# Softmax division folded into the transposition of the probabilities: a diagonal matrix as the moving operand of a matmul

## The reference, cut to what matters

```
def fox_mix(u, q_norm_g, k_norm_g, fgate_b):
...
    for blk in range(s // BLOCK_Q):
        s0, s1 = blk * BLOCK_Q, (blk + 1) * BLOCK_Q
        scores = jnp.einsum('bqhd,bkhd->bhqk', q[:, s0:s1], k[:, :s1]) * scale
        bias = c[:, :, s0:s1, None] - c[:, :, None, :s1]
        causal = jnp.arange(s1)[None, :] <= (s0 + jnp.arange(BLOCK_Q))[:, None]
        scores = jnp.where(causal, scores + bias, -jnp.inf)
        probs = jax.nn.softmax(scores, axis=-1)
        outs.append(jnp.einsum('bhqk,bkhd->bqhd', probs, v[:, :s1]))
```

## Time and profile before

| | |
|---|---|
| median of 3 runs | 2901.72 us (2898.87 to 2904.9) |
| the profiled execution's own time | 2899.26 us |
| its span | 2897.3 us |
| mean granted TensorE clock | 0.985 of 2.4 GHz |
| busy | PE 2782.7 us (96%), DVE 1161.8 (40%), ACT 1001.3 (35%), POOL 216.3 (7%) |

### The profile page before, as it was taken

The page is one execution under the profiler, slowest core; times in us unless marked ns, Lnnn a source line. Parts: engine busy times, 40 slices in busy tenths (PEclk is TensorE's granted clock), DMA queues, the critical chain, the costliest instruction groups (busy, mean ns, idle before and its releaser), DMA issues.

```text
span 2897.3 us, 41123 instructions
## 1 busy us (share of the span) xinstructions
PE 2782.7 (96%) x15562; PEld 2206.9 (76%) x15562; DVE 1161.8 (40%) x1677; ACT 1001.3 (35%) x1388; POOL 216.3 (7%) x343
## 2 busy tenths in 40 slices
PE   7989998998998979999999999999999999999998
PEld 5777676666666747888888888888888888888787
DVE  6643652553453343333333333333333333334544
ACT  5433533433442333343322333223332222233521
POOL 2100110120120011100000000000000000001300
PEclk9999999999999989999999999999999999999999
DMA  4221121112113104222223332233222322223332
GB/s 159 87 67 55 56 78 51 62 51 81 48 60 87 67 30 162 99 102 94 99 83 97 106 100 95 84 97 108 94 94 85 103 101 99 97 82 100 104 123 76
DMA packets 107733, 255.33 MB, mean 88 GB/s; under 512 B 35657, under 2 KB 37193, under 8 KB 107625
## 3 DMA queue, kind: packets, MB, share of 16 engines
q1 hardware_dynamic: 106352, 249.73, 26.9%
q0 software_dynamic: 1280, 4.20, 0.4%
HBM read 244.90 MB, written 8.98 MB: 88 GB/s over the span
## 4 chain that ended last, share of the span: by engine, by line
issue 75%; PE 14%; POOL 3%; DVE 2%; ACT 1%; SPq 0%; DMA 0%; POOLq 0%; DVEq 0%; ACTq 0%
PE bank L288 4%; PE bank L285 4%; PE bank L289 3%; PE bank L320 2%; POOL probs L971 1%; POOL scratch_pool L116 1%; SPq L1187 0%; DVE w_lo L280 0%; PE bank L470 0%; DMA solved_scratch<-solved 0%; POOL acc_e L1740 0%; POOL carried L994 0%; POOL sg_t L963 0%; POOL M_t L980 0%; PE bank L442 0%
## 5 line engine op out<-in xcount | busy, mean ns | idle before, releaser
L280 DVE TENSOR_TENSOR w_lo<-raw,w_hi 128x1024 fp32r<-128x1024 f32 (+1 forms) x476 | 541.8, 1140 | 963.5 <-ACT w_hi L273 953.5
L273 ACT ACTIVATE w_hi<-raw 128x1024 fp32r<-128x1024 f32 (+1 forms) x476 | 468.2, 987 | 1044.5 <-PE bank L289 999.2
L285 PE MATMUL bank<-hn_hi,w_hi 128*128 128x512 f32 x1664 | 648.1, 389 | 0.0
L289 PE MATMUL bank<-hn_hi,w_lo 128*128 128x512 f32 x1664 | 647.3, 389 | 0.0
L288 PE MATMUL bank<-hn_lo,w_hi 128*128 128x512 f32 x1664 | 647.3, 389 | 0.0
L285 PE MATMUL bank<-in_hi,w_hi 128*128 128x512 f32 x1086 | 467.3, 430 | 55.2 <-DMA T_t<-solved_scratch 31.2
L288 PE MATMUL bank<-in_lo,w_hi 128*128 128x512 f32 x1086 | 442.4, 407 | 0.0
L289 PE MATMUL bank<-in_hi,w_lo 128*128 128x512 f32 x1086 | 428.8, 395 | 0.0
L288 PEld LDWEIGHTS bank<-hn_lo,w_hi 128*128 128x128 f32 x1664 | 312.4, 188 | 65.3 <-issue 0.5
L285 PEld LDWEIGHTS bank<-hn_hi,w_hi 128*128 128x128 f32 x1664 | 312.4, 188 | 65.1 <-issue 0.5
L289 PEld LDWEIGHTS bank<-hn_hi,w_lo 128*128 128x128 f32 x1664 | 312.4, 188 | 64.9
(11 more groups left out here) (233 smaller groups left out, 2161.7 us busy)
## 6 DMA issues: line engine op xcount, KB each, us to landing
raw<-w_gu SPq DMA_DIRECT2D x176, 512.0 KB, 3.4
raw<-w_mix SPq DMA_DIRECT2D x136, 512.0 KB, 3.6
raw<-w_down SPq DMA_DIRECT2D x64, 384.0 KB, 3.1
raw<-w_down SPq DMA_DIRECT2D x64, 320.0 KB, 2.8
raw<-ple_gate SPq DMA_DIRECT2D x32, 512.0 KB, 3.5
x_raw<-xT SPq DMA_DIRECT2D x4, 1024.0 KB, 11.6
h_t<-xT SPq DMA_DIRECT2D x4, 1024.0 KB, 8.8
out<-h_t POOLq DMA_DIRECT2D x16, 256.0 KB, 2.3
```

What stands on the lines that cost most here:

```text
L273: nc.scalar.activation(w_hi[:, ring_slots(par2, half), 0:cols[half]], raw[:, half, 0:cols[half]], ACT.Copy).then_inc(hi_ready, 1)
L280: nc.vector.tensor_tensor(w_lo[:, s, 0:cols[half]], raw[:, half, 0:cols[half]], w_hi[:, s, 0:cols[half]].bitcast(F32), ALU.subtract).then_ ...
L285: nc.tensor.matmul(out, w_h, x_hi, start=start, stop=False, skip_group_check=True)
L289: return nc.tensor.matmul(out, w_l, x_hi, start=False, stop=stop, skip_group_check=True)
```

## The change

The DVE, right behind the reciprocal, writes `shares`: the identity times the reciprocals, one per row, so a 128x128 matrix with the reciprocal row sums on its diagonal (doubled, `q % 2`). The PE multiplies each block of unscaled probabilities by it in an ordinary float32 matmul where it transposed against the identity: the block is the stationary operand as before, and `shares` takes the identity's place as the moving one. The scaling on Pool is gone, in the groups and behind them. Nothing else is moved; line numbers from L204 on shift by one or more.

```
+    shares = sb("shares", [P, 2, P])
...
-            pe.wait_ge(S("probs_normed"), 16 * gp + q + 1)
+            pe.wait_ge(S("shares_ready"), 16 * gp + q + 1)
...
-                last = nc.tensor.transpose(pt_bank[q % 2][:, tok(kb)], probs[:, q % 2, tok(kb)], const(C_ID))
+                last = nc.tensor.matmul(pt_bank[q % 2][:, tok(kb)], probs[:, q % 2, tok(kb)], shares[:, q % 2, :],
+                                        start=True, stop=True)
...
             nc.vector.reciprocal(small[:, 12 + q % 2:13 + q % 2], small[:, 10 + q % 2:11 + q % 2]
                                  ).then_inc(S("rsum_ready"), 1)
+            dve.wait_ge(S("rsum_ready"), 16 * gp + q + 1)
+            if q >= 2:
+                dve.wait_ge(S("probs_turned"), 16 * gp + q - 1)
+            nc.vector.tensor_scalar(shares[:, q % 2, :], const(C_ID), small[:, 12 + q % 2:13 + q % 2], None, ALU.mult
+                                    ).then_inc(S("shares_ready"), 1)
...
-    def pool_attention(pool, s, kt, gp):
-        q = attention_item(s, kt, "scale")
-        if q is not None:
-            n = (q % TT + 1) * P
-            pool.wait_ge(S("rsum_ready"), 16 * gp + q + 1)
-            own_wait(pool, 1 + q % 2)
-            nc.gpsimd.tensor_scalar(probs[:, q % 2, 0:n], probs[:, q % 2, 0:n], small[:, 12 + q % 2:13 + q % 2],
-                                    1.0, ALU.mult, ALU.mult).then_inc(S("probs_normed"), 1)
```

More of the change, by code:

```diff
@@ L1709, in group @@
                         if s < 6:
-                            if gp is not None:
-                                pool_attention(pool, s, kt, gp)
                             pool_rwkv_prep(pool, s, kt, g)
@@ L1718, in _ @@
             group_loop(pool, group)
-            for s in range(6):
-                for kt in range(KT):
-                    pool_attention(pool, s, kt, GROUPS - 1)
             pool.wait_ge(S("in_ready"), 2 * KT)
```

## The result

| | before | after |
|---|---|---|
| median of 12 runs each, us | 2901.64 (2898.87 to 2904.9) | 2907.91 (2902.45 to 2911.08) |
| ratio, 95% interval | 1 | 1.0019 (1.0011 to 1.0027) |
| profiled execution, us | 2899.26 | 2907.97 |
| its span, us | 2897.3 | 2906.3 |

The changed kernel is slower by 5.5 us by the ratio: just inside the 0.2% that was called no difference, while the whole interval lies above 1. The forecast was +5.1 and 2906.8.

The account below looks back on a forecast made before the run. The PE, busy 96% of the span, was taken to bound the kernel. Added work 16.2, less 8.0 and 1.45 of waits and 1.6 of clock, gave +5.1 us: 2906.8 against the median 2901.72, range 2898 to 2915.

Parts of the forecast that it names:

- The price of a block: PE's turn: a 128x128 block as ordinary float32 product costs 0.215 us against 0.11 transposed, 0.105 more per block.
- Rival 1: PE's turn: the product costs no more than the transposition, 0.11 per block; -11.1 us, 2890.7; chance 0.06.
- rival 2: PE's turn: weight loads don't overlap, a block costs up to 0.39; +32 (2934), or 2914 at 0.26; chance 0.10.
- rival 3: PE's turn: a block costs four times the transposition, 0.44; +40 us, 2942; chance 0.04.
- The term of the sum: Work added on the PE: 149 blocks at 0.105 give 15.6, six at half clock +0.6; 16.2 us.
- Items 5 and 15: Turns in each attention group: the PE's waits go away entirely, giving back 0.66 and 1.60 us.
- the 8.0 of the forecast: Waits given back in the three attention groups: 2.68 us each, at items 1, 5 and 15; 8.0 us.
- my 1.45: Waits given back in the tail: 0.4 at item 1, 0.4 at item 13, 0.65 at item 15; 1.45 us.
- Item 1: Turn in each attention group: the DVE is late behind the RWKV group norm, so the 2.65 us wait gives only 0.42.
- The tail's long wait: Tail, in front of item 1: the 9.58 us wait stays almost whole, near 8.8, as the DVE is late there too.
- The clock: PE behind item 1's wait: of two groups' falls to half clock, one goes, giving back 1.6 us (bounds 0 and 3.2).
- The fifth rival: PE clock: both falls in the groups and the one at the tail's end go; +0.9 us, 2902.6; chance 0.10.

Follow-up runs that it names:

- e2: The changed kernel with the transposition put back, `shares` built and waited for but division left out: 2895.54 us, 0.9978 of the kernel before.
- e4: The changed kernel with a second build of `shares` into a spare tile, the PE waiting for that one: 2910.57 us, 1.0030 of the kernel before.
- e10: The kernel before with scaling on the DVE instead of Pool, transposition kept, Pool's clears held behind item 15's scaling: 2894.29 us, 0.9968.
- e1: The kernel before with the turn as an ordinary product with the identity, Pool's scaling kept: 2916.53 us, 1.0046.
- e11: The kernel before with DVE scaling, later clears, and the group norm by Ln and Exp on ACT: 2884.03 us, 0.9926.
- e12: The changed kernel with Pool's clears later and the group norm by Ln and Exp on ACT: 2893.49 us, 0.9959 of the kernel before.

## Why the prediction was right, point by point

- **The price of a block** was forecast as 0.215 from L355 and came out as 0.225. Rival 1 (0.11), rival 2 (0.26 and up) and rival 3 (0.44) are ruled out, by the distances and by the product alone. The term of the sum was 16.2; at 0.225 it is 149 x 0.115 + 0.7 = 17.8. The work that came in is 16.2 us in the stretch and 18.2 on the page of the whole span; where they part is open.
- **The rule of four.** By what the Trainium skill says (TensorE: Matmul & The Clock Gate, Terms) a block would have come to 0.44. The factor is 2 here (0.225 / 0.11): the measurement decides.
- **Items 5 and 15** lost their waits, as forecast. With item 1 the listed waits of the groups fell by 7.4 in all (the 8.0 of the forecast is counted by distances between starts), and those of the tail from 12.88 to 10.43, by 2.45. That is more than my 1.45: 0.6 of it because the longer products of items 0, 12 and 14 now fill a part of these waits, where I had left those blocks out of the work instead, and 0.4 because I had taken item 1's gain at half.
- **Item 1** was forecast at a wait of 2.2 put to the DVE, and is 2.08; the start 0.51 after the reciprocal is 0.53. **The tail's long wait** was forecast near 8.8 and is 8.66.
- **`shares`** was taken as 0.24 by a straight line between two shapes and takes 0.29. The error of 0.05 went under, because I had allowed 0.11 for two hand-overs and they need less.
- **The clock** was to give back 1.6. This step failed: it gave back nothing at item 1, where two of three groups fall as before, and 0.3 in the whole stretch (25.7 and 25.0 us of work at the low clock). That a wait shorter by 0.42 makes the fall rarer is not borne out. Behind waits of 2.24 us one group of three falls (e2), behind 2.3 one (e4) or all three (e10), behind 2.5 two (e1). Only where that wait is gone (e11, e12) does none fall there. The fifth rival, that the clock recovers, falls too: item 15 of the tail takes 1.92 for four blocks, where it takes 1.06 in a group.
- **What the sum lacked** was a gain of the opposite sign. The waits of the values shrank from 4.6 to 3.4, because the products in front of them are longer: 1.2 us of the new work hides in a wait that I did not list. The chain is turn, copy by ACT, values; it ends in a different line from the one that the change touches. With it and without the clock my terms make 17.8 - 8.0 - 1.45 - 1.2 = +7.1. Page and waits say the same: +18.2 of work, less 9.9 and 1.2 of waits, is +7.1. The medians say +5.5 to +6.3, the stretch +5.2; the 1 to 2 us between are open.
- **The two halves.** By the runs the product alone is +13.3 and Pool's removal alone -6.4, together +6.9 where the change is +5.5: they add within the uncertainty. But each is smaller than my term for it (16.2, and 9.45 without the clock), and the errors have opposite signs. For the product the cause is shown: it also fills waits that the other half removes. For the removal it is shown too: Pool's clears move up and meet the DVE, which costs 4.6 of waits. I had looked at what is queued behind a wait that is added, and not at what was queued behind the work that is removed, although the diff of the order showed it. In the change this meeting was short and stayed hidden; with `shares` built twice it was long in two groups of three, so in other executions of the change it may be long too, which no trace here shows. So the forecast was right in its mechanism: the doubled price of a block against the waits one by one. Its time, within 1.1 us of the measured one, owes something to luck. The work was taken 1.6 too low, and the clock gain of 1.6 did not come; against these two stand 1.2 of filled waits that the sum left out, and 1 to 2 us more that are open.

## What to carry to other kernels

A wait named after the last engine of a chain is worth only that engine's own link: of 26.6 us that stood against Pool, 8 to 10 went with Pool's scaling, and moving work about in the DVE's queue behind the rest only gave the wait another name, while taking a long instruction out of that queue gave 12 us (0.9968 to 0.9926). When work is taken off an in-order queue, look at what stood behind it: it moves up, and may now meet someone. And on a PE that is busy 96% of the time, a product that replaces a transposition pays for each of its blocks, so here a cheap multiplication on the DVE, which is busy 40% of the time and one hand-over away, wins (2896.18 against 2907.91).

## What the runs showed of the hardware

- A float32 product of 128x128 by 128 columns costs 0.225 us back to back and the transposition of the same block 0.11, although the weight loads are recorded with a mean of 197 ns each, two for each block, in the product, and with 143 ns, one for each block, in the transposition. Two loads in a row would make 0.39, so they overlap with each other or with the products. By the column the short product costs about 4% more than L355 with 512 columns (0.225 against 0.217).
- A DVE instruction of 128x128 (0.29 us) that starts 1.38 us behind eight clears on Pool can take 2.48 us or 0.61, both in one execution, and takes 0.29 again when the clears are held back. The clears take 3.79 us in the first case and 3.86 to 3.94 in the second.
- A dependent instruction on the DVE starts 0.19 behind a one-column reciprocal (303.17, 303.36), and a second build 0.20 behind the first one, before that one's 0.29 are over.
- The DVE's reciprocal of 128x512 takes 3.35 us; the logarithm and the exponential of that size on ACT take 0.68 and 0.62, with four table loads of 1.28 for either line. Groups of instructions in the fastest kernel (count, us in total, mean ns):

```profile
L666 ACT ACT_TABLE_LOAD x4 | 5.1, 1283 | 0.1
L670 ACT ACT_TABLE_LOAD x4 | 5.1, 1283 | 0.1
L666 ACT ACTIVATE t<-bank,ccol 128x512 f32<-128x512 f32 x8 | 5.1, 684 | 0.0
L670 ACT ACTIVATE t<-t 128x512 f32<-128x512 f32 x8 | 4.6, 622 | 0.0
```
